# Recurrent products moved off GpSimd, the `conv` tiles spread over two units, and the first layer's squares taken slice by slice

## The reference, cut to what matters

```python
u = rms_norm(x, norm_g)
p = u @ w_in
qk, v, o, z_a, ig, fg, xb, z_b = jnp.split(p, SPLIT_AT, axis=-1)
...
xc = causal_dwconv(xb, lru_conv_w) + lru_conv_b            # width 4
# rg_lru:
r = sigmoid(per_head(xc, w_a) + b_a)
i = sigmoid(per_head(xc, w_x) + b_x)
log_a = -8.0 * r * softplus(-lam)
a = exp(log_a)
u = xc * i * sqrt(-expm1(2.0 * log_a))
h_t = a_t * h_(t-1) + u_t
y_b = h * silu(z_b)
x = x + jnp.concatenate([y_a, y_b], axis=-1) @ w_out
```

## Time and profile before

| | |
|---|---|
| median of 3 runs | 3134.16 us (3132.17 to 3136.26) |
| the profiled execution | 3129.72 us, its span 3128.0 us |
| granted clock of PE, mean over the span | 0.982 |
| busy: PE, VectorE, ScalarE, GpSimd | 95%, 62%, 52%, 6% of the span |
| first layer's units 0 to 11 | 1511 to 1850 us from the span's start |
| second layer's units 0 to 11 | 2320 to 2645 us |

### The profile page before, as it was taken

How to read it: one execution, slowest core, us unless ns; L and a number is a source line. 1 busy time by engine, 2 the same in 40 slices (tenths; PEclk the granted TensorE clock), 3 DMA queues, 4 the chain that set the end, 5 groups by cost and what they waited for, 6 DMA issues and landing times.

```text
span 3128.0 us, 41355 instructions
## 1 busy us (share of the span) xinstructions
PE 2967.4 (95%) x16791; PEld 2592.4 (83%) x16791; DVE 1952.4 (62%) x2228; ACT 1627.3 (52%) x1942; POOL 175.1 (6%) x111
## 2 busy tenths in 40 slices
PE   4799999999889999999899999999999999999998
PEld 3798998899767777777789998888889999888886
DVE  4557644544478888888675775555556668555554
ACT  3354444444367777777645544445444563445443
POOL 0403100000000000000001100000000010000000
PEclk8899999999989999999999999999999999999999
DMA  4454556554569898989544456555564455555553
GB/s 152 130 180 139 203 184 242 198 179 162 163 215 325 305 338 297 347 287 358 192 162 163 155 168 202 176 180 171 186 204 149 148 176 189 175 175 175 178 185 135
DMA packets 322919, 629.31 MB, mean 201 GB/s; under 512 B 18441, under 2 KB 28210, under 8 KB 321330
## 3 DMA queue, kind: packets, MB, share of 16 engines
q1 hardware_dynamic: 319776, 617.03, 58.2%
q10 hardware_dynamic: 2674, 8.67, 0.7%
q0 software_dynamic: 288, 1.05, 0.1%
HBM read 619.37 MB, written 7.34 MB: 200 GB/s over the span
## 4 chain that ended last, share of the span: by engine, by line
PE 72%; DVE 11%; ACT 7%; issue 5%; DMA 5%; ACTq 0%; DVEq 0%; POOL 0%; SPq 0%; POOLq 0%
PE pairs L614 14%; PE pairs L616 14%; PE pairs L615 14%; PE pairs L624 7%; PE pairs L626 7%; PE pairs L628 7%; DVE w_lo L1797 6%; ACT w_hi L1279 3%; PE misc L1011 2%; DMA raw<-in_w_gate_dram 2%; DMA raw<-in_w_down_dram 1%; DMA raw<-in_w_up_dram 1%; PE misc L906 1%; PE misc L741 1%; PE misc L950 1%
## 5 line engine op out<-in xcount | busy, mean ns | idle before, releaser
L1797 DVE TENSOR_TENSOR w_lo<-raw,w_hi 128x1024 fp32r<-128x1024 f32 x1136 | 1405.4, 1260 | 905.8 <-ACT w_hi L1279 899.2
L1279 ACT ACTIVATE w_hi<-raw 128x1024 fp32r<-128x1024 f32 x1136 | 1178.0, 1058 | 998.1 <-PE pairs L616 580.9
L614 PE MATMUL pairs<-w_hi,a_hi 128*128 128x512 f32 x1664 | 661.5, 398 | 17.8 <-DVE w_lo L1797 15.7
L616 PE MATMUL pairs<-w_hi,a_lo 128*128 128x512 f32 x1664 | 649.8, 390 | 0.0
L615 PE MATMUL pairs<-w_lo,a_hi 128*128 128x512 f32 x1664 | 649.6, 390 | 0.0
L624 PE MATMUL pairs<-a_hi,w_hi 128*128 128x256 f32 x1920 | 560.9, 292 | 63.9 <-DVE w_lo L1797 63.9
L626 PE MATMUL pairs<-a_lo,w_hi 128*128 128x256 f32 x1920 | 552.9, 288 | 0.0
L628 PE MATMUL pairs<-a_hi,w_lo 128*128 128x256 f32 x1920 | 552.4, 288 | 0.0
L624 PEld LDWEIGHTS pairs<-a_hi,w_hi 128*128 128x128 f32 x1920 | 378.4, 197 | 70.7 <-DVE w_lo L1797 41.8
L614 PEld LDWEIGHTS pairs<-w_hi,a_hi 128*128 128x128 f32 x1664 | 313.3, 188 | 97.7 <-DVE w_lo L1797 26.7
L626 PEld LDWEIGHTS pairs<-a_lo,w_hi 128*128 128x128 f32 x1920 | 378.7, 197 | 0.7 <-issue 0.2
...
## 6 DMA issues: line engine op xcount, KB each, us to landing
...
```

What stands on the lines that cost most here:

```text
L614: nc.tensor.matmul(o, hi[:, k, tok], w_hi[:, s, q, :], start=k == 0, stop=False)
L616: m = nc.tensor.matmul(o, lo[:, k, tok], w_hi[:, s, q, :], start=False, stop=last)
L1279: a.activation(w_hi[:, i % HSLOTS], raw[:, i // 2, 2 * (i % 2):2 * (i % 2) + 2, :], ACT.Copy).then_inc(hi_done, 1)
L1797: v.tensor_tensor(w_lo[:, i % HSLOTS], raw[:, i // 2, 2 * (i % 2):2 * (i % 2) + 2, :], w_hi[:, i % HSLOTS].bitcast(F32), ALU.subtract).the ...
```

## The change

It has three parts. GpSimd's three products for each group move: `Ib` (`gated_input`) and `Zb` (`gated_output`) to VectorE, the square `Rb` to ScalarE, behind `exps`. The chain of a group is laid out anew: two of the four `conv` tiles move from the odd unit to the next even one, `sigmoids` and `exps` move from halves 6 and 7 to 8 and to half 1 of the next unit, `root`, `recur`, `y_hi`, `y_lo`, `qk_silu`, `rows_v` and `rows_2` move with them. The squares between the networks are taken earlier and in wider pieces, and the norm's small operations and `scale_rows` are spread over several halves.

```diff
+        xg_low = sc(8208, TT, 3 * COLS)
+        xg_top = sc(5120, TT, COLS)
+        xg = [xg_low[:, :, j * COLS:(j + 1) * COLS] for j in range(3)] + [xg_top]
+        junk_low = sc(2048, 3 * COLS)
...
@@ PE
                     if n == 1:
-                        hooks = {3: lambda: rows_out(l)}
+                        hooks = {1: lambda: rows_out(l)}
@@ GpSimd
-                for j in range(4):
-                    n = 4 * l + j
-                    pool.wait_ge(gates_ok, n + 1)
-                    g.tensor_tensor(Ib, xc, Ib, ALU.mult).then_inc(ui_ok, 1)
-                    pool.wait_ge(at_ok, n + 1)
-                    g.tensor_tensor(Rb, Ab, Ab, ALU.mult).then_inc(a2_ok, 1)
-                    pool.wait_ge(h_ok, n + 1)
-                    pool.wait_ge(z_ok, n + 1)
-                    g.tensor_tensor(Zb, Rb, Zb, ALU.mult).then_inc(y_ok, 1)
@@ ScalarE
+                def low_squares(src, T, out, to):
+                    if step.n:
+                        step.wait()
+                    step(a.activation(out, src[:, T, 0:3 * COLS], ACT.Square, accum_out=to[:, T, 0:1]))
+                def x_low(T):
+                    if T == 0:
+                        act.wait_ge(var_ok, 4)
+                        act.wait_ge(x_added, 4 * (GROUPS - 1) + 3)
+                    low_squares(x, T, junk_low, sq_part)
+                def xg_squares(T):
+                    if T == 0:
+                        act.wait_ge(xg_ok, 3)
+                    low_squares(xg_low, T, junk_low, sq_gain)
...
                 if m_ == 0 and l == 0:
+                    todo[0].append(lambda: x_low(0))
+                    todo[1].append(lambda: x_low(1))
+                    todo[2].append(lambda: xg_squares(0))
                     todo[3].append(moe_rest)
+                    todo[4].append(lambda: xg_squares(1))
                     todo[5].append(lambda: split_hi(4, 3, a_hi, "norm0"))
-                    todo[7].append(final_squares)
+                    todo[6].append(x_top)
+                    todo[7].append(xg_top_squares)
...
                     m.then_inc(at_ok, 1)
+                    act.wait_ge(at_ok, 4 * l + j + 1)
+                    a.activation(Rb, Ab, ACT.Square).then_inc(a2_ok, 1)
...
-                    todo[3].append(lambda: z_silu(j))
-                    todo[6].append(lambda: sigmoids(j))
-                    todo[7].append(lambda: exps(j))
+                    todo[5].append(lambda: z_silu(j))
+                    todo[8].append(lambda: sigmoids(j))
                 if 3 <= m_ <= 9 and m_ % 2 == 1:
                     j = (m_ - 3) // 2
-                    todo[2].append(lambda: root(j))
-                    todo[7].append(lambda: y_hi(j))
+                    todo[1].append(lambda: exps(j))
+                    todo[4].append(lambda: root(j))
+                    todo[8].append(lambda: y_hi(j))
                 if 10 <= m_ <= 13:
-                    todo[1].append(lambda: qk_silu(m_ - 10))
+                    todo[4].append(lambda: qk_silu(m_ - 10))
...
-                        todo[4].append(rows_2)
+                        todo[6].append(rows_2)
@@ VectorE
+            def gated_input(l, j):
+                n = 4 * l + j
+                dve.wait_ge(gates_ok, n + 1)
+                v.tensor_tensor(Ib, xc, Ib, ALU.mult).then_inc(ui_ok, 1)
+            def gated_output(l, j):
+                n = 4 * l + j
+                dve.wait_ge(h_ok, n + 1)
+                dve.wait_ge(z_ok, n + 1)
+                v.tensor_tensor(Zb, Rb, Zb, ALU.mult).then_inc(y_ok, 1)
...
                     if m_ == 0 and l == 0:
+                        for j in range(3):
+                            todo[j].append(lambda j=j: gained(j))
                         todo[3].append(moe_rest)
                         todo[5].append(lambda: split_lo(4, 3, a_hi, a_lo, "norm0"))
-                        for j in range(4):
-                            todo[6 + j // 2].append(lambda j=j: gained(j))
+                        todo[6].append(lambda: gained(3))
...
                     if m_ == 1:
-                        todo[3].append(lambda: layer_scale(l))
-                        todo[5].append(lambda: scale_row(l))
+                        if l == 0:
+                            todo[0].append(final_variance)
+                            todo[1].append(gained_variance)
+                        else:
+                            todo[0].append(lambda: variance(6))
+                        todo[2].append(lambda: layer_scale(l))
+                        todo[6].append(lambda: scale_row(l))
                     if m_ == 2 and l == 0:
-                        todo[0].append(lambda: scale_rows(r_one, gain_b, 1))
+                        todo[4].append(lambda: scale_rows(r_one, gain_b, 1, [0]))
+                        todo[5].append(lambda: scale_rows(r_one, gain_b, 1, [1]))
                     if m_ <= 7 and m_ % 2 == 1 or 9 <= m_ <= 12:
                         i = m_ // 2 if m_ <= 7 else m_ - 5
-                        todo[5 if m_ == 1 else 3].append(lambda: pad_in(l, i))
-                        for f in range(4):
-                            todo[min(f + (5 if m_ == 1 else 4), 8)].append(lambda f=f: conv_tile(l, i, f))
+                        at = 6 if i == 0 else 3
+                        one, two = (7, 8) if i == 0 else (4, 6) if i <= 4 else (5, 7)
+                        todo[at].append(lambda i=i: pad_in(l, i))
+                        todo[one].append(lambda i=i: conv_tile(l, i, 0))
+                        todo[two].append(lambda i=i: conv_tile(l, i, 1))
+                    if 2 <= m_ <= 8 and m_ % 2 == 0 or 10 <= m_ <= 13:
+                        i = m_ // 2 - 1 if m_ <= 8 else m_ - 6
+                        todo[1].append(lambda i=i: conv_tile(l, i, 2))
+                        todo[2].append(lambda i=i: conv_tile(l, i, 3))
...
                         j = (m_ - 3) // 2
-                        todo[1].append(lambda: one_minus_a2(l, j))
-                        todo[3].append(lambda: recur(l, j))
-                        todo[8].append(lambda: y_lo(l, j))
+                        todo[1].append(lambda j=j: gated_input(l, j))
+                        todo[2].append(lambda j=j: one_minus_a2(l, j))
+                        todo[5].append(lambda j=j: recur(l, j))
+                        todo[7].append(lambda j=j: gated_output(l, j))
+                    if 4 <= m_ <= 10 and m_ % 2 == 0:
+                        todo[0].append(lambda: y_lo(l, (m_ - 4) // 2))
...
-                        todo[1].append(lambda: rows_v(l))
+                        todo[3].append(lambda: rows_v(l))
```

56 lines of the change are left out of this document (30 added, 26 removed).

## The result

The changed kernel takes **3100.77 us** (median of four runs, 3099.14 to 3104.63) against 3135.18 us (3132.17 to 3136.26) for the kernel before: a ratio of 0.9889, 95% interval 0.9875 to 0.9904, or 34.4 us less. Its profiled execution took 3104.63 us, with a span of 3102.6. In this kernel's lines the weight remainder is L1820, the feature products start at L627, the gate products are L1014, the spread behind half 0.0 is L953, and `conv_tile` is L2373 and L2379.

A forecast was written before the change was run, and what follows sets the result against it. PE, at 95% of the span, was taken as the bound. Gains of 3.8 + 8.7 + 3.9 + 7.0 + 8.3 - 0.6 = 31.1 us, off the median of 3134.16, gave 3103 us, range 3092 to 3118.

The forecast's parts named there:

- The bound, and where to look: Whole kernel: PE, at 95% of the span, is the bound; only its waits and slow running can be saved.
- The 51 us of excess: Recurrent stages of both layers: measured less nominal PE time, 51.1 us, the most the change can win.
- The steady pair: Pairs of units, 2.3 to 10.0: new waits of 7.1 us a layer, so gains of 7.0 and 8.3 us.
- Half o.5: Half 5 of a pair's odd unit: PE starts it 0.80 us late, its `w_lo` standing behind `recur`.
- the gate wait: Before the next even unit's gate products: PE waits 0.94 us for the fourth `conv` tile, three times a layer.
- The short waits get no slow clock: Steady pairs: the new short waits, 0.8 and 0.9 us, are given no fall of the clock.
- Products and places: Steady pairs: moved products (2 x 1.13 us on VectorE, 0.97 on ScalarE) and new places walked together, no separate gains.
- Units 1 and 2: Stretch 1.0 to 2.3: scale, pad and `conv` spread over halves 1.6 to 2.2 leave no wait; gain 8.7 and 3.9 us.
- Unit 0: First layer, 0.0 to 1.0: copy behind wide squares makes L950 3.6 us late, slow clock 1.6 more; gain 3.8 us.
- The rival on larger squares: Unit 0, first layer: 512-wide squares would win 9.0 us instead of 3.8; without unit 0's gain, total 27; no chance given.
- Units 12 and 13: End of each layer's stage: moved `rows_v` and tiles delay half 13.3 by about 0.3 us; loss 0.6 in all.
- The gain taken from the median: Whole kernel: 31.1 us taken from the median of the runs, 3134.16 us, giving 3103 us.

The follow-up runs named there:

- three_moves: Kernel of copy_first with VectorE's `y_lo` moved behind the next unit's fourth `conv` tile and ScalarE's `y_hi` behind the weight split of half 1: 3092.43 us.
- conv_twice: Changed kernel with VectorE computing the fourth `conv` tile twice in units 4, 6, 8 and 10 of each layer: 3127.11 us.
- y_later: Changed kernel with VectorE's `y_lo` taken behind the fourth `conv` tile of the next unit instead of ahead of its third: 3103.42 us.
- pool_back: Changed kernel with the three products of each group back on GpSimd, everything else in its new place: 3120.33 us.
- products_only: Kernel before with only the three products moved to VectorE and ScalarE, in the old places: 3139.25 us.
- unit1_back: Changed kernel with VectorE's work of units 1 and 2 back where it stood before, in both layers; `rows_out` stays early: 3104.96 us.
- copy_first: Changed kernel with ScalarE's copy of the mixture's last pair ahead of the first wide square over the gained slices, in unit 0: 3098.55 us.
- after_again: Changed kernel, unchanged, run once more for a second profile: 3101.32 us (a single run).
- narrow_squares: Kernel of copy_first with the squares of the first layer's norm over 512 columns each again, at the same places: 3100.09 us.
- before_again: Kernel before, unchanged, run once more for a second profile: 3139.39 us (a single run).

## Why the prediction was right

The forecast, 3103 us, lies 2 us above the median, and all stretches but one came within 0.1 us. By its steps:

- **The bound, and where to look**: right. All of the gain lies in PE's waits and in the clock behind them. The 51 us of excess that it set as the most that could be won stand against 34 won, and 42 in three_moves.
- **The steady pair**: right in place, slightly high in size. Half o.5 was 0.66 late, not 0.80; o.6 0.14 and o.1 0.13, as worked out; the gate wait 0.90 to 0.92 for 0.94, six times. The sums of 7.0 and 8.3 us were exact by some luck: halves o.2 and o.7, each 0.1 late and not in the walk, made up for o.5. conv_twice, y_later and three_moves show that the gate wait is VectorE's lateness for the fourth tile, one to one.
- **The short waits get no slow clock**: right. None of the changed kernel's waits up to 0.7 us in the two stages was followed by one, in three traces, nor was the 1.2 before 12.7.
- **Products and places**: the prediction walked them as one and had no term for either. pool_back and products_only show that they could not have been added up: by itself each is worth between 0.6 and -1.8 us a layer in the pairs, together 8.3.
- **Units 1 and 2**: right in size, 8.6 and 3.8 for 8.7 and 3.9, with a reason that is incomplete at least. The step in question is "scale, pad and `conv` spread over halves 1.6 to 2.2". unit1_back shows that, with the rows brought earlier, this is worth 1.55 us in the first layer and nothing in the second. The prediction read the long waits there as VectorE's work in a lump and missed the 6.71 us for which VectorE itself had been waiting; of the moved `rows_out` it said nothing. The spread may have been enough by itself, as the estimate above has it, but no run shows that, so in these 12.4 us the agreement of the sizes confirms no reason.
- **Unit 0**: the mechanism was right, and copy_first shows it: without the square in front the stretch is 25.68. Two sizes were off. The wait was 3.0 instead of 3.6 us, since the copy came 5.0 us after PE's start, not 5.4. The slow clock cost 2.8 us in the profiled execution (1.4 in half 0.0, 1.4 in 0.1) where 1.6 stood in the sum, and 1.4 in after_again, each held against the 28.96 us of conv_twice. So the gain was 2.9 there and 4.1 in after_again, for 3.8. The rival on larger squares, in which unit 0 would win nothing, fell: the wide ones are the better ones, by 0.6 us in narrow_squares.
- **Units 12 and 13**: 0.42 to 0.46 us lost a layer for 0.3; half 13.3 is 0.3 late, as foretold, and takes 0.13 longer itself.
- **The gain taken from the median**: 31.1 foretold, 34.4 measured. Part of the 3.3 between may be the slow clock of the kernel before: before_again lost 2.5 us more to it in the five stretches than the trace from which the prediction was made. How much an average run loses, no trace shows, and 3 us are within the spread of the runs.
